# One VectorE subtraction of 2048 columns for two weight units, in a diffusion layer kernel

## What is computed

```python
x = x + 0.5 * g1 * swiglu(modulate(rms_norm(x, w1), sh1, sc1), ffn1_wi, ffn1_wo)
z = modulate(rms_norm(x, w2), sh2, sc2) @ w_in      # q, k, v, gates of an mLSTM and of an attention
mix = (sigmoid(gate_m) * (mlstm(z) @ w_proj_m) + sigmoid(gate_a) * (attention(z) @ w_proj_a)) @ w_out
x = x + g2 * mix
x = x + 0.5 * g3 * swiglu(modulate(rms_norm(x, w3), sh3, sc3), ffn2_wi, ffn2_wo)
```

## Time and profile before

| | |
|---|---|
| median of 3 runs | 2222.83 us (2222.77 to 2223.15) |
| profiled execution, its span from first to last instruction | 2220.9 us |
| PE busy | 2187.9 us, 99% of the span |
| DVE busy | 1634.8 us, 74% |
| ACT busy | 936.0 us, 42% |
| mean granted TensorE clock | 0.998 of full speed |

### The profile page before, as it was taken

The page is one execution under the profiler, slowest core; times in us unless marked ns, Lnnn a source line. Parts: engine busy times, 40 slices in busy tenths (PEclk is TensorE's granted clock), DMA queues, the critical chain, the costliest instruction groups (busy, mean ns, idle before and its releaser), DMA issues.

```text
span 2220.9 us, 28326 instructions
## 1 busy us (share of the span) xinstructions
PE 2187.9 (99%) x10448; PEld 1752.6 (79%) x10448; DVE 1634.8 (74%) x1881; ACT 936.0 (42%) x1098; POOL 64.5 (3%) x55
## 2 busy tenths in 40 slices
PE   6999999999999999999999999999999999999999
PEld 3568777777777778888888888888888888888887
DVE  3447888888888889756767888984577676776856
ACT  3333333333333346455554344464443444344443
POOL 0001000000000000001500000100000000000000
PEclk9999999999999999999999999999999999999999
DMA  9999888788888876555536776846665757567573
GB/s 364 387 369 307 286 315 314 270 293 290 306 301 283 281 262 222 198 171 170 186 114 228 269 254 233 278 159 207 228 227 190 264 189 264 189 195 259 188 228 132
DMA packets 273332, 548.13 MB, mean 247 GB/s; under 512 B 9014, under 2 KB 9418, under 8 KB 273008
## 3 DMA queue, kind: packets, MB, share of 16 engines
q1 hardware_dynamic: 212676, 423.69, 55.9%
q10 hardware_dynamic: 57484, 113.47, 14.2%
q0 software_dynamic: 3104, 10.05, 1.6%
HBM read 543.71 MB, written 3.46 MB: 246 GB/s over the span
## 4 chain that ended last, share of the span: by engine, by line
PE 94%; DVE 3%; DMA 1%; issue 1%; ACT 1%; SPq 0%; DVEq 0%; ACTq 0%
PE ps L697 29%; PE ps L699 29%; PE ps L698 29%; PE ps L638 1%; PE ps L623 1%; DMA ada_w_sb<-in_ada_w 1%; PE ps L774 1%; DVE w_lo L1789 1%; DVE acc L2003 0%; PE ps L1091 0%; PE ps L684 0%; PE ps L1159 0%; PE ps L1167 0%; DVE xm L1909 0%; ACT w_hi L1338 0%
## 5 line engine op out<-in xcount | busy, mean ns | idle before, releaser
L1338 ACT CAST w_hi<-raw_w 128x1024 fp32r<-128x1024 f32 x728 | 764.8, 1053 | 1162.2 <-PE ps L699 1114.1
L1789 DVE TENSOR_TENSOR w_lo<-raw_w,w_hi 128x1024 fp32r<-128x1024 f32 x728 | 896.5, 1235 | 405.3 <-ACT w_hi L1338 402.2
L697 PE MATMUL ps<-w_hi,xT_hi 128*128 128x512 f32 x2080 | 821.8, 395 | 5.6 <-DVE xT_lo L1877 4.2
L699 PE MATMUL ps<-w_hi,xT_lo 128*128 128x512 f32 x2080 | 811.1, 390 | 0.0
L698 PE MATMUL ps<-w_lo,xT_hi 128*128 128x512 f32 x2080 | 810.8, 390 | 0.0
L697 PEld LDWEIGHTS ps<-w_hi,xT_hi 128*128 128x128 f32 x2080 | 391.0, 188 | 110.2 <-issue 24.6
L699 PEld LDWEIGHTS ps<-w_hi,xT_lo 128*128 128x128 f32 x2080 | 391.0, 188 | 83.0
L698 PEld LDWEIGHTS ps<-w_lo,xT_hi 128*128 128x128 f32 x2080 | 391.3, 188 | 78.8
L1849 DVE SCALAR_TENSOR_TENSOR vec_acc<-ada_w_sb,ctile,vec_acc 128x512 f32<-128x512 f32 x420 | 299.0, 745 | 0.0
L697 PE MATMUL ps<-w_hi,hT_hi 128*128 128x512 f32 x704 | 276.4, 393 | 0.0
L699 PE MATMUL ps<-w_hi,hT_lo 128*128 128x512 f32 x704 | 274.3, 390 | 0.0
(11 more groups left out here) (277 smaller groups left out, 1037.8 us busy)
## 6 DMA issues: line engine op xcount, KB each, us to landing
raw_w<-in_ffn_wi SPq DMA_DIRECT2D x176, 1024.0 KB, 5.1
ada_w_sb<-in_ada_w ACTq DMA_DIRECT2D x96, 1024.0 KB, 8.3
raw_w<-in_ffn_wo SPq DMA_DIRECT2D x88, 1024.0 KB, 5.3
raw_w<-in_w_in SPq DMA_DIRECT2D x68, 1024.0 KB, 5.3
ada_w_sb<-in_ada_w SPq DMA_DIRECT2D x30, 1024.0 KB, 12.8
raw_w<-in_w_out SPq DMA_DIRECT2D x16, 1024.0 KB, 5.3
ada_m<-in_ada_w ACTq DMA_DIRECT2D x12, 1024.0 KB, 5.5
raw_w<-in_w_proj_m SPq DMA_DIRECT2D x8, 1024.0 KB, 5.3
```

What stands on the lines that cost most here:

```text
L697: pe.matmul(out, a_hi, w_hi[:, slot, kk, :], start=(first and kk == 0), stop=False)
L699: mm = pe.matmul(out, a_lo, w_hi[:, slot, kk, :], start=False, stop=(last and kk == 1))
L1338: act.copy(w_hi[:, us % SPL, :, :], raw_w[:, slot, 2 * half:2 * half + 2, :]).then_inc(hi_ready, 1)
L1789: dve.tensor_tensor(w_lo[:, us % SPL, :, :], raw_w[:, slot, 2 * half:2 * half + 2, :], w_hi[:, us % SPL, :, :].bitcast(F32), ALU.subtract) ...
```

## The change

DVE's `split` does nothing for an even unit. For an odd unit it waits for this unit's `hi_ready` and subtracts the whole tile, both its units, in one instruction of 2048 columns, which then raises `lo_ready` by 2. ACT, PE, SP and GpSimd run the same instructions as before, with the same waits.

```diff
                 if isinstance(ux, int) and us + ux >= U_END:
                     return
-                slot, half = (us // 2) % RAW, us % 2
+                if us % 2 == 0:
+                    return
+                at = us % SPL - 1
                 dve.wait_ge(hi_ready, us + ux + 1)
-                dve.tensor_tensor(w_lo[:, us % SPL, :, :], raw_w[:, slot, 2 * half:2 * half + 2, :],
-                                  w_hi[:, us % SPL, :, :].bitcast(F32), ALU.subtract).then_inc(lo_ready, 1)
+                dve.tensor_tensor(w_lo[:, at:at + 2, :, :].rearrange("p u k n -> p (u k n)"),
+                                  raw_w[:, (us // 2) % RAW, :, :].rearrange("p k n -> p (k n)"),
+                                  w_hi[:, at:at + 2, :, :].bitcast(F32).rearrange("p u k n -> p (u k n)"),
+                                  ALU.subtract).then_inc(lo_ready, 2)
```

## The result

| | before | after |
|---|---|---|
| median | 2222.89 us (4 runs) | 2260.99 us (4 runs, 2259.52 to 2264.10) |
| span of the profiled execution | 2220.9 us | 2257.5 us |

The ratio is 1.0173, with a 95% interval of 1.0161 to 1.0185: 1.7% slower. The forecast was 2252 us, +1.3%, and its range ended at 2260, 1 us short. The sign and the places were right; the sum was too small, 29.1 us for the span against 36.6.

A forecast was written before the change was run, and what follows sets the result against it. TensorE, busy 2187.9 of 2220.9 us, was taken as the bound. Late places summed to 26.2 us, plus 2.9 for the clock: 29.1, giving a 2250.0 span, plus 1.9 around it: 2252 us, range 2236 to 2260.

The forecast's parts named there:

- The named places: Prologue units 0, 6, 16, 22, norms, GpSimd's stretch, FFN ends, `w_out`, mLSTM: late pairs, 0.2 to 4.4 us each.
- the stretch beside GpSimd: Units 326 and 327, where GpSimd's work stretches DVE's subtractions: the pair 2.9 us late, lower bound 1.9.
- unit 262: Last units of the first FFN: pair taken as 0.9 us late like unit 726's, 1.7 for both FFNs.
- the mLSTM: A chain of small DVE steps there comes 1.07 us later, against a wait of 0.9 it eats: 0.2.
- The 0.05 that each has for the semaphore: At each late place, 0.05 us added after the pair's 2.30 us subtraction, before TensorE's start of the even unit.
- That leaves 1.8 us, still free: FFN loop: pair done at +3.58, even unit wanted at +5.44, so no loss; cover was 5.6 us before.
- The rival of the thin cover: FFN loops: a long instruction of 3.3 us makes pairs late, 14 us more, 2266; chance 0.10 (above 2260).
- Whether it comes I can't read from one case; I count one of the two: 2.9: Clock: stands before units 6 and 22 may each bring half rate, 0 to 3.4 us; one counted, 2.9.
- The trace has no other stand of this length: Clock: no stand like the 4.8 us foreseen before units 6 and 22, so each may bring a half-rate stretch.
- the upper end of the range: Whole kernel: 2260 us, covering both slow stretches of the clock plus the bounds of the uncertain places.
- The 22 to 29 us: DVE time saved over the kernel, at 0.06 to 0.08 us a pair; nearly none on TensorE's path.
- little of it counts: Rival: only the prologue's loss hides and unseen slips cover half the other places: +4 us; chance 0.04.

The follow-up runs named there:

- kernel with filled stands: Changed kernel plus matmuls nobody reads while TensorE would stand before units 6, 16, 22 and 464; 2255.34 us, ratio 1.0145 to the kernel before.
- profile with 3 sums: Kernel with the pair in the FFNs' regular flow alone, plus 3 unread DVE sums ahead of one pair per second-FFN step; 2240.84 us, 1.0079 of before.

## Why the prediction was wrong

**The direction, the mechanism and the places were right.** The even unit waits for the odd one's rounding, and in the prologue, at the norms and beside GpSimd's work that is 2 to 5 us too late. The named places measured within 0.4 us of their terms, but for the stretch beside GpSimd (3.7 for 2.9), unit 262 (1.8 for 0.9) and the mLSTM (1.1 for 0.2). The 0.05 that each has for the semaphore is short by 0.1 at six of them: from the end of the subtraction to TensorE's first matmul the changed kernel's trace has 0.15 us before units 0, 6, 16, 22, 264 and 464, and 0.05 to 0.06 before its other late units. The waits on `w_lo` are there (14 of them, some 10 forecast), and the kernels with single subtractions at these places take the loss away again.

**Loops.** "That leaves 1.8 us, still free" was right to the hundredth (1.80), and the step's length didn't grow. The rival of the thin cover was right about the size of the cover, and wrong about the instruction.

**The step that failed: the clock.** "Whether it comes I can't read from one case; I count one of the two: 2.9." Both stands of 5 us brought a slow stretch, and two more came after stands that the prediction foresaw but for which it charged nothing of the clock, 2.27 us before unit 16 and 2.99 before unit 464. The term measured 7.0 in place of 2.9 (2.2 and 2.0 at the long stands, 1.7 and 1.4 at the two others, less 0.3 at unit 0), and the kernel with filled stands shows 5.8 us of the loss to be clock alone even though two others came up in it.

So a stretch was dearer in the prediction than it is, and their number too small: both long stands at 2.9 each would have given 2255, still 6 us short. The sentence "The trace has no other stand of this length" was true once TensorE had begun, but the upper end of the range held only one stretch more than the forecast. With the 1.7 and 1.4 us of the two others its end would have lain at 2263, past the result. Both long stands were to be charged: unit 0's shorter one, 3.38 us, had brought half rate in the trace before, and in the runs 11 of 11 stands of 4.4 us do. For the stands of 2 to 3 us no run here gives a rule: 2 of 11 at 2.1 us, and at unit 264 (2.99) full rate in both profiles of the changed kernel, half rate in three of the experiments. Why one such stand brings a slow stretch and its like doesn't stays open.

**The smaller misses, 3.4 us more in all.** I took unit 262 from unit 726, but there the pair's rounding was done at 863.8, and the pair itself began only at 864.65, behind two instructions on the gated output. In the mLSTM I priced one chain at 0.2; two small results, `lf` and `scan`, stand behind longer instructions, and TensorE's waits for them grew from 0.3 in all to 2.4, of which one wait of 0.9 that goes pays back a part. Delays too small for a pair-by-pair list made up 1.7 (unit 343 and the steps under 0.25). Against them stand 2.1 us that I hadn't credited, waits of TensorE for `ada_w` and for `ada_rows_sb` before unit 252 that a late TensorE, or a freer DVE, shortens.

**The part on gains.** Nothing of DVE's 48.5 us reached TensorE beyond those waits. The 22 to 29 us that I had put down for DVE were too few: 0.06 to 0.08 us a pair holds where two subtractions stand side by side, but in the loops DVE waits between them, and there 242 pairs saved 32.3 us, 0.13 each. The size of the gain was wrong by half, and it didn't matter. In the rival "little of it counts" the sum was off: half of the 11.5 outside the prologue is nearly 6, not 4.

**Length and place.** The kernel with two subtractions at the odd place parts the two: of 38 us, 11.4 are the larger instruction, and 26.5 its later place, with the slow stretches that this brings.

## What to carry to other kernels

Merging two instructions of a producer means that the first half waits for the inputs of the second: look for the places where those inputs stand behind other work, not at the average cover in the loop. If the merge is wanted, move the inputs up with it, and keep single instructions at the edges; and if the engine isn't the bound, as DVE isn't here at 74%, expect little for the work saved: 32.3 us of it in the loops brought 0.6. When a change makes TensorE stand for several microseconds, charge the slow clock after each stand (here 29 of 29 of 3.4 us and more brought it, and those whose cost was read took 1.5 to 2.6 us), and give the shorter stands a chance of it in the range (7 of 9 of 2.99 us, 6 of 19 of 2.1 to 2.3).

## What the runs showed of the hardware

- Stands of TensorE of 4.4 us brought half rate in 11 of 11 cases, of 4.98 in all four of the changed kernel's two profiles. Over all twelve profiles, from 20 us on, each of the 29 stands of 3.4 us and more brought it, 7 of 9 of 2.99, 6 of 19 of 2.1 to 2.3 (2 of the 11 set up for it), 1 of 2 of 1.92, and 1 of 33 of 1.4 to 1.7 (1.59 us before unit 20, in the profile with 3 sums). The same stand of 2.99 us, before unit 264, was followed by half rate in some kernels and not in others, with the same instructions around it. Behind these stands half rate lasted 3.4, 6.8 or 10.2 us, at the late units most of it with TensorE at work, and in the case of unit 16 it began half a microsecond after work had been taken up again (windows of 120 to 124 us: 3.96 us busy at a mean clock of 0.57).
- Matmuls that nobody reads kept the granted clock at 1.00 through the changed kernel's stands before units 6, 16, 22 and 464. They cost nothing there: units 6, 16 and 22 started late by the same amounts to 0.01 us.
- At full clock a matmul of 512 columns in fp32r starts 0.227 us after the one before it and has a record of 0.39 us, in a slow stretch 0.427 and 0.63. In float32 its record is 0.59 us (line 1159, kernel before).
- In the kernel before, 10 of the 728 subtractions take more than 1.3 us, up to 3.43. All ten lie between 1058 and 1094 us, beside GpSimd's additions and products (its line 570 runs from 1057.21 for 5.22 us); those with no work of GpSimd beside them take 1.23 at most.
- A subtraction of 2048 columns takes 2.30 us for 1.235 of one of 1024, so its fixed part is near 0.17 us; but neighbouring single ones overlap (three in 3.50). Of DVE's busy time 48.5 us went with 364 instructions, 0.13 each.
